# Front norms before the front's transposes, gt2's columns in the up loop, and the first merge products in the memory steps

## The reference

```
mod = silu(c) @ w_ada + b_ada                 -> shift, scale, gate (gt1, gt2) for two sub-layers
h   = rmsnorm(x) * (1 + sc1) + sh1
proj = h @ w_in + b_in                        -> xin, bg, cg, q, k, v, o, ig, fg, gate_c, gate_m
conv branch:   y = bg * dwconv3(cg * xin);  p_conv = y @ w_proj_conv
memory branch: mLSTM over chunks of 128, 4 heads (key 128, value 256), head norm, sigmoid(o) * hm,
               p_mlstm = ... @ w_proj_mlstm
z = sigmoid(gate_c) * p_conv + sigmoid(gate_m) * p_mlstm;   x = x + gt1 * (z @ w_out)
h = rmsnorm(x) * (1 + sc2) + sh2
x = x + gt2 * ((silu(dwconv3(h @ w_up_a)) * (h @ w_up_g)) @ w_down)     (d_ff = 2816)
out = rmsnorm(x) * g_final
```

## Time and profile before

| | us |
|---|---|
| median of 3 runs | 1341.28 (1341.21 to 1413.05) |
| profiled execution | 1341.2 |
| its span, core 2, the slowest | 1339.8 |
| spans of the eight cores | 1330.5 to 1339.8 |
| TensorE busy on core 2 | 1258.8 (94%) |
| VectorE, ScalarE busy | 679.4 (51%), 533.3 (40%) |

### The profile page before, as it was taken

The page is one execution under the profiler, slowest core; times in us unless marked ns, Lnnn a source line. Parts: engine busy times, 40 slices in busy tenths (PEclk is TensorE's granted clock), DMA queues, the critical chain, the costliest instruction groups (busy, mean ns, idle before and its releaser), DMA issues.

```text
span 1339.8 us, 21446 instructions; the slowest of 8 cores (1330.5 to 1339.8 us)
## 1 busy us (share of the span) xinstructions
PE 1258.8 (94%) x7694; PEld 689.0 (51%) x7694; DVE 679.4 (51%) x1241; ACT 533.3 (40%) x1069; POOL 86.1 (6%) x165
## 2 busy tenths in 40 slices
PE   1878999999899999999999999899999999999997
PEld 1445455666556655666654444445544444444443
DVE  1463342577733356666655423478632465655534
ACT  2554113765422235444443331566421255544212
POOL 3100000000100000000000000000000000000000
PEclk9998999999989999999999999999999999999999
DMA  8987025378684375334274673323627274432502
GB/s 140 163 206 122 0 40 94 54 114 135 104 188 64 63 146 107 64 63 80 40 182 75 159 145 63 64 32 64 134 56 126 44 139 77 88 64 41 101 16 110
DMA packets 35287, 126.19 MB, mean 94 GB/s; under 512 B 2796, under 2 KB 3052, under 8 KB 35184
## 3 DMA queue, kind: packets, MB, share of 16 engines
q0 software_dynamic: 27248, 97.93, 43.4%
q1 hardware_dynamic: 7936, 26.90, 5.8%
HBM read 214.34 MB, written 8.39 MB: 166 GB/s over the span
## 4 chain that ended last, share of the span: by engine, by line
PE 84%; DMA 6%; DVE 4%; issue 3%; ACT 2%; POOL 0%; DVEq 0%; ACTq 0%; SPq 0%; POOLq 0%
PE psum L548 56%; PE psum L1384 11%; PE psum L1231 4%; PE psum L890 4%; DMA arena<-xin 4%; PE psum L1500 2%; DVE arena L1079 1%; PE psum L507 1%; DMA xt<-xin 1%; DMA arena<-bada_row 1%; PE psum L753 1%; PE psum L952 1%; ACT sqj L458 1%; PE psum L954 0%; PE psum L963 0%
## 5 line engine op out<-in xcount | busy, mean ns | idle before, releaser
L548 PE MATMUL psum<-arena,wslot 128*128 128x512 bf16 (+1 forms) x4640 | 830.1, 338 | 7.7 <-DVE arena L1016 5.0
L548 PEld LDWEIGHTS psum<-arena,wslot 128*128 128x128 bf16 x4640 | 451.2, 98 | 356.8 <-issue 19.5
L1305 DVE SCALAR_TENSOR_TENSOR arena<-arena,pcol_t 128x1028 f32<-128x1028 f32 (+1 forms) x88 | 113.2, 1287 | 93.0 <-ACT arena L1302 88.5
L1384 PE MATMUL psum<-wslot,arena 128*128 128x512 bf16 x704 | 152.8, 379 | 1.7 <-ACT arena L528 1.7
L1167 ACT ACTIVATE arena<-psum,pcol_t 128x512 bf16<-128x512 f32 (+1 forms) x80 | 47.8, 603 | 162.6 <-PE psum L548 161.5
L1384 PEld LDWEIGHTS psum<-wslot,arena 128*128 128x128 bf16 x704 | 68.8, 98 | 84.0 <-issue 1.9
L1307 ACT ACTIVATE arena<-arena 128x1028 f32<-128x1028 f32 (+1 forms) x44 | 46.6, 1059 | 121.0 <-DVE arena L1305 121.0
L458 ACT ACTIVATE sqj<-arena 128x1024 bf16<-128x1024 f32 x40 | 42.2, 1055 | 93.2 <-DVE arena L1387 53.1
L1179 DVE TENSOR_TENSOR arena<-psum,arena 128x512 f32<-128x512 f32 (+1 forms) x40 | 23.4, 585 | 83.0 <-PE psum L548 82.1
L1231 PE MATMUL psum<-wslot,arena 128*128 128x512 bf16 (+1 forms) x272 | 60.3, 379 | 0.2 <-DVE arena L532 0.2
L890 PE MATMUL psum<-wslot,arena 128*128 128x512 bf16 (+1 forms) x272 | 59.3, 379 | 0.0
(11 more groups left out here) (201 smaller groups left out, 1095.9 us busy)
## 6 DMA issues: line engine op xcount, KB each, us to landing
wslot<-w_in POOLq DMA_DIRECT2D x32, 1024.0 KB, 11.9
arena<-xin SPq DMA_DIRECT2D x25, 512.0 KB, 16.4
wslot<-w_ada POOLq DMA_DIRECT2D x12, 1024.0 KB, 15.0
wslot<-w_up_a POOLq DMA_DIRECT2D x10, 1024.0 KB, 9.5
wslot<-w_up_g POOLq DMA_DIRECT2D x10, 1024.0 KB, 11.6
wslot<-w_down POOLq DMA_DIRECT2D x8, 1024.0 KB, 9.1
y<-arena SPq DMA_DIRECT2D x15, 512.0 KB, 2.7
wslot<-w_proj_conv POOLq DMA_DIRECT2D x4, 1024.0 KB, 13.9
```

The lines of the kernel that those rows point to most:

```text
L548: S.op("pe", lambda e: e.matmul(psum[:, b, 0:n], lhsT=wv[:, k, wcol0:wcol0 + 128], rhs=src[:, k, t0:t0 + n], start=(k == 0), stop=(k == 7) ...
L1305: S.op("dve", lambda e: e.scalar_tensor_tensor(out=t3[:, T0:NT], in0=a_s[:, s_ + T0:s_ + NT], scalar=pcol[:, cw + s_:cw + s_ + 1], in1=t3[ ...
L1384: S.op("pe", lambda e: e.matmul(psum[:, b, :], lhsT=act_t[jj][:, t0:t0 + 128], rhs=wv[:, jj % 8, :], start=(jj == 0), stop=(jj == NFF - 1) ...
```

## The change

Four moves; no product, evacuation or transfer of the computation is added or taken away.

1. Front: norms of the first stage's tiles are asked for later in the prefix loop (0 at c = 11 instead of 10, two each at c = 13 and 14), and inside an iteration behind `tgroup` rather than ahead of it. A fifth buffer `xfr` takes tile 8, so that all nine norms stand ahead of the three groups' transposes; `act_every` goes back to its default of 2 (four blocks of eight on each engine).
2. `sdb` is copied right after `stage_gates(0)` instead of after the prefix's gates.
3. gt2's two `ada_bcast` leave the units of the middle and run in the up loop after j = 6 and j = 10, with a bias buffer of their own. Row biases are loaded ahead: the first before the units (or at j = 1 of the up loop), the second right after the first is used.
4. `merge_conv(0)` and `merge_gate(0)` become units at the end of the chain, so the last chunk's D steps stand among them. `nblk` falls from 80 to 78 in the first stage, as the two `ada_bcast` left it, and stays 48 in the second.

```diff
-        def ada_bcast(n, dst, r_dst, half):
+        def load_bada(n, badabc, r_bada):
+            row0 = n % 2 * 512 + (0 if n < 6 else 1024)
+            S.dma("sp", badabc, badar_d[:, row0:row0 + 512].partition_broadcast(128), writes=[r_bada])
+
+        def ada_bcast(n, dst, r_dst, half, badabc=badabc, r_bada=r_bada):
             si = load_w("ada", n * T)
-            row0 = half * 512 + (0 if n < 6 else 1024)
-            S.dma("sp", badabc, badar_d[:, row0:row0 + 512].partition_broadcast(128), writes=[r_bada])
...
             free_w(si)
+            if half == 0:
+                load_bada(n + 1, badabc, r_bada)
...
-            t_, r_ = (xnb[f], r_xnb[f]) if f < 4 else (xfr[f - 4], r_xfr[f - 4]) if f < 8 else (xnb[0], r_xnb[0])
+            t_, r_ = (xnb[f], r_xnb[f]) if f < 4 else (xfr[f - 4], r_xfr[f - 4])
...
         for c in range(NPF):
-            norm_upto((0, 0, 0, 0, 0, 0, 0, 0, 0, 0, 1, 2, 3, 4, 5, 6)[c])
             sumsq(*squares.get(c, ()))
             if c in (3, 7, 11):
                 tgroup(c // 4 + 1)
+            norm_upto((0, 0, 0, 0, 0, 0, 0, 0, 0, 0, 0, 1, 2, 4, 6, 7)[c])
             b = kproj(c)
...
+            def merge_conv(j):
+                sg, zc, r_s, r_c = sg_t[j % 2], zc_t[j % 2], r_sg[j % 2], r_zc[j % 2]
+                if j == 0:
+                    S.reuse(r_sg + r_zc, [r_xs, r_u, r_t3] + r_sgf)
...
+                yield from proj_blocks(mt["gc"], (j % 4) * 128, hT, rd_h, tbs, merge_ev_g(j, 32))
+                yield from proj_blocks(mt["pc"], (j % 4) * 128, ycT, lambda k, t0, n: [r_yc[k]], tbs, ev_pc)
...
             S.reuse([r_bada], hooks["F"])
+            if first:
+                load_bada(4, badabc, r_bada)
             units = [unit_x(0), unit_c(0)]
             for j in range(1, 8):
-                units += [unit_x(j), unit_b(j - 1)] + ([unit_ada(j + 3)] if first else []) + [unit_c(j)]
-            units += ([unit_ada(11)] if first else []) + [unit_b(7)]
-            nblk = 24 * len(tbs) + (8 if first else 0)
+                units += [unit_x(j), unit_b(j - 1)] + ([unit_ada(j + 3)] if first and j < 7 else []) + [unit_c(j)]
+            units += [unit_b(7)]
+            units += [merge_conv(0), merge_gate(0)]
+            nblk = 24 * len(tbs) + (6 if first else 0)
...
-            for fn, j in [(merge_conv, 0), (merge_gate, 0), (merge_conv, 1), (merge_mem, 0), (merge_gate, 1), (merge_mem, 1)]:
-                fn(j)
+            drain(merge_conv(1))
+            merge_mem(0)
+            drain(merge_gate(1))
+            merge_mem(1)
...
                 if j == 1:
+                    if first:
+                        S.reuse([r_bada2], r_yc)
+                        load_bada(10, badabc2, r_bada2)
...
+                if first and j in (6, 10):
+                    i = (j - 6) // 4
+                    ada_bcast(10 + i, gt2bc, r_gt2, i, badabc2, r_bada2)
                 if j in (17, 19, 21):
                     dn_tile(0)
...
+        norm_upto(9)
         for g in range(3):
             tiles = front_tiles[g * 3:g * 3 + 3]
-            transp(tiles, hT, LAY[0][0][g * 3][0], r_h0[g], G1, r_G1, SH1, 3)
-            norm_upto(9)
+            transp(tiles, hT, LAY[0][0][g * 3][0], r_h0[g], G1, r_G1, SH1)
         allow_w(1 << 30, r_xt[xbuf[8]])
         stage_gates(0, r_h0)
+        r_sdb = Res("sdb")
+        S.reuse([r_sdb], [r_shbc])
+        S.op("dve", lambda e: e.tensor_copy(out=sdb, in_=...), reads=r_sdP, writes=[r_sdb])
```

More of the change, by code:

```diff
@@ L285, in _build @@
         shhl = sb("shhl", [128, 16], BF16)
-        xfr = [at("E", 8192 + i * 2048, [128, D], BF16) for i in range(4)]
+        xfr = [at("E", 8192 + i * 2048, [128, D], BF16) for i in range(4)] + [at("F", 20480, [128, D], BF16)]
         r_wslot = RL("wslot", NSLOT)
@@ L1108, in unit_ada, with drain, merge_ev_g, f @@
                 yield
+            def drain(*gens):
+                gens = list(gens)
+                while gens:
+                    for g_ in list(gens):
+                        try:
+                            next(g_)
+                        except StopIteration:
+                            gens.remove(g_)
+            r_sg, r_zc = RL("sg", 2), RL("zc", 2)
+            si_w = []
+            mt = {}
+            def merge_ev_g(j, col):
+                def f(b, t0, n):
+                    S.op("act", lambda e: e.activation(out=sg_t[j % 2][:, t0:t0 + n], in_=psum[:, b, 0:n], func=AF.Sigmoid,
+                                                       bias=pcol[:, PC_B + col + j:PC_B + col + j + 1]),
+                         reads=[r_bank[b], r_pc], writes=[r_sg[j % 2]])
+                return f
@@ new lines, in merge_gate @@
+            def merge_gate(j):
+                yield from proj_blocks(mt["gm"], (j % 4) * 128, hT, rd_h, tbs, merge_ev_g(j, 40))
+                if j in (6, 7):
+                    i = j - 6
+                    si_w.append(load_w("out", i * T))
+                    S.op("dve", lambda e: e.tensor_tensor(out=wslot[si_w[i]][:], in0=wslot[si_w[i]][:],
+                                                          in1=gt1bc[:, i * 512:(i + 1) * 512].rearrange("p (o n) -> p o n", o=1).to_broadcast([128, 8, 512]),
+                                                          op=ALU.mult), reads=[r_wslot[si_w[i]], r_gt1], writes=[r_wslot[si_w[i]]])
@@ new lines, in merge_mem, with ev_pm @@
+            def merge_mem(j):
+                sg, zc, r_s, r_c = sg_t[j % 2], zc_t[j % 2], r_sg[j % 2], r_zc[j % 2]
+                def ev_pm(b, t0, n):
+                    S.op("dve", lambda e: e.tensor_tensor(out=sg[:, t0:t0 + n], in0=psum[:, b, 0:n], in1=sg[:, t0:t0 + n], op=ALU.mult),
+                         reads=[r_bank[b], r_s], writes=[r_s])
+                    S.op("dve", lambda e: e.tensor_tensor(out=zT[:, j, t0:t0 + n], in0=sg[:, t0:t0 + n], in1=zc[:, t0:t0 + n], op=ALU.add),
+                         reads=[r_s, r_c], writes=[r_z[j][tbi(t0, n)[0]]])
+                proj(mt["pm"], (j % 4) * 128, sgoT, lambda k, t0, n: [r_hm[c] for c in hit(chunks, t0, n)], tbs, ev_pm)
+                if j % 4 == 3:
+                    free_w(mt["gm"], mt["pm"])
@@ L1162, in run_stage @@
             ask_res(0, 6)
[L1163 to L1183, removed]
-                    free_w(mt["gc"], mt["pc"])
-                if j == 7:
-                    ask_res(6, 8)
@@ L1252, in transp2 @@
                 yield from transp_blocks(tiles2[g], hT, chunks[groups[g][0]][0], r_h2[g], G2, r_G2, SH2)
-            def drain(*gens):
-                gens = list(gens)
-                while gens:
-                    for g_ in list(gens):
-                        try:
-                            next(g_)
-                        except StopIteration:
-                            gens.remove(g_)
             rest = list(groups[2])
@@ L1492, in _build @@
         r_MT, r_nsb, r_shn = RL("MT", 8), Res("nsb"), RL("shn", 2)
-        S.reuse(r_MT + [r_nsb] + r_shn, [r for i in range(2) for r in r_hTp[i]] + [r_shbc])
+        S.reuse(r_MT + [r_nsb] + r_shn, [r for i in range(2) for r in r_hTp[i]] + [r_shbc, r_xfr[4]])
         passes = [[(0, None), (1, 0), (2, 1), (3, 2), (4, 3)], [(5, 4), (6, 5), (7, 6), (0, 7)]]
```

48 lines of the change are left out of this document (17 added, 31 removed).

## The result

The changed kernel takes 1331.3 us (median of 4 runs, 1330.2 to 1332.9) against 1341.3 for the kernel before; the ratio is 0.9928, 95% interval 0.9916 to 0.9941, so 9.7 us less. The forecast was 14.9 us less, 1326.3. The measured time is inside the range given (1320 to 1335), and inside the 2% to which the chances referred; but the gain is two thirds of the sum: the terms of the front and of the memory steps were mis-sized, and `sdb` gave what was forecast only where TensorE's clock was low. Two of the four runs of the kernel before fell in the chip's slower state (1380.5 and 1413.1 us) and are left out of the ratio.

The account below looks back on a forecast made before the run. TensorE, nearly full behind the front, was taken as the bound, so only its idle time could be given back; VectorE ended the front. 5.5 + 0.6 + 6.7 + 2.1 = 14.9 us off 1341.2 gave 1326.3, range 1320 to 1335.

Parts of the forecast that it names:

- part 1: Front: later norms and three evacuations moved to ScalarE end it at 100.4 instead of 105.9 us, a gain of 5.5 us.
- the products for q start 0.4 us behind: End of the front: q's products follow VectorE's end by 0.4 us, as at 106.31 after 105.9 us before.
- part 4: First stage's middle: with `nblk` 78 for 80, TensorE's waits at memory steps fall from 8.0 to 6.0, gain 2.1 us.
- the wait at X of chunk 6: First stage's middle, a memory step: TensorE gets a wait of 0.8 us there in the new order.
- part 2: The `sdb` copy, moved ahead of the prefix gates, is covered by q's first products: 0.6 us gained, bounds 0 and 1.2.
- What bounds: Whole kernel: TensorE is nearly full behind the front, so only its idle time can be given back; VectorE ends the front.
- Part 3, the bias row: End of the middle: TensorE's 5.0 us wait goes, plus 1.7 for the clock, together 6.7 us.
- The bank count: End of the middle: banks come free in time for `unit_b(7)`, D steps and merge blocks, with 0.2 us to spare.
- The part 3 rival: End of the middle: VectorE still behind from the convolution, a 2 us wait and the clock's fall stay: 1329.9; chance 0.10.
- The front stays DMA-paced: Front: tiles 2 to 5 land no sooner, so it gives 0.9 instead of 5.5 us: 1330.9; chance 0.14.
- Four banks: Merge: each of 15 blocks waits 0.6 to 0.7 us for an evacuation, 10 us in all: 1336.3; chance 0.05.
- VectorE becomes the bound of the middle: Middle: every D waits 3.17 and every X 1.89 us, 40.5 where 8.0 were: 1360.9; chance 0.03.

Follow-up runs that it names:

- the weights held back: Changed kernel, but POOL asks for the next weights only after the front's last evacuation, not when the last x tile has landed: 0.9910 to the kernel before.
- the front alone: Kernel before with move 1 alone (norms later and behind the prefix's transposes, fifth buffer, evacuations shared 12 to 12): 0.9983.
- rows-ahead experiment: Kernel before with only the row biases loaded ahead and modulation unit 10 put ahead of 9: 0.9969.
- the last kernel: Changed kernel with late weights, norms behind `kevac`, and A, K and the root 0.04 of a chunk earlier in both stages: 0.9862 to the kernel before, 1323.5 us.
- the experiment with the old spacing: Changed kernel with the first stage's memory steps spread over 80 blocks instead of 78: 0.9931 to the kernel before.
- one tile for four: Changed kernel with one weight tile asked for when the last x tile has landed, the other three after the front's last evacuation: 0.9919 to the kernel before.

## Why the prediction was right and wrong, point by point

The steps that failed are these. In part 1 it is "the products for q start 0.4 us behind" VectorE: 5.5 us forecast, 3.5 measured on core 2, since TensorE stood there for its instructions. In part 4 it is the wait at X of chunk 6, where ScalarE's queue was not followed: 2.1 us forecast, a loss of 1.0 measured. In part 2 it is the cover of the copy, which is short by 0.9 us where TensorE runs at full clock.

**What bounds.** Right. TensorE's time behind the front passes on: out to down is the same but for the 3.46 us moved, and down to end within 0.8 us in the mean.

**Part 1, the front: 5.5 forecast, 3.5 on core 2, 2.5 in the mean.** VectorE's sum was right within 1 us: its work of 24.3 and its idle time of 3.0 gave an end at 100.4; to 99.8 it was busy 23.4 us and idle 3.3, and its last evacuation ended at 99.7. The failed step is "the products for q start 0.4 us behind it". Here 3.1 us lie between on core 2, and 2.7 to 3.9 on the seven cores with the pause, but 0.6 on core 4, which has none: TensorE's instruction block is late, and it was late in no row of before, where TensorE came to its place after it. With the weights held back q starts 0.8 us sooner in the mean, and on core 2 at 100.8, which is the forecast's 106.31 - 5.5; the ratio falls by 0.0018, 2.4 us, but that run's interval overlaps the changed kernel's. So of this term the pauses are shown and the microseconds only roughly. Means of q's start over several kernels with one front say the same: 105.5 for the old front (104.5, 105.5 and 106.5), 102.6 for the new one with the weights early (102.0, 102.8, 103.1 and 102.7), 101.4 with them held back (101.2 and 101.6). The Trainium skill (Runtime: NRT & Kernel Launch, Instruction fetch mechanics) says that instructions come in blocks of 16 KiB, fetched by DMA while the block before runs, and that the cost of crossing from one to the next is mostly hidden. The packets of 16 KB agree; that it stays hidden does not hold in this front, with 1.5 to 3.3 us between two products on seven of eight cores.

A second error is in taking core 2 for the chip. It had the latest q of all (106.31 against 102.85 to 105.42), so it had the most to gain, and the time is the slowest core's. After the change core 6 sets it, with 1329.6 for core 2's 1328.7.

**Part 2, sdb: 0.6.** Right for core 2, and not for the kernel as such: TensorE's wait before the state products is 2.06 us for 2.65, and no loss of cover shows there (the 0.9 for `gm_logf` in core 2's list is at 165.8 us, and stood there before). But it shows where q's products run at full clock (1.00 from q to state), which in the changed kernel is core 4 alone:

```profile
104.47 0.41 PE L583 MATMUL psum<-gm_logf,maskf 128*128 128x64 f32 x2 [0.89 <-DVE gm_logf L578]
```

This is VectorE's gate operation behind the copy. With the weights held back six cores wait so, 0.89 to 1.05 us. From q to state it is 25.88 us on core 4, where the front alone, with the copy in its old place, has 25.35 on four cores. So at full clock the move loses 0.5 us, outside the bounds of 0 and 1.2, and its 0.6 here is in part luck: q's products were slow because TensorE had just stood. No run puts the copy back in the kernels with the weights held back, where that should pay.

Not forecast either: core 2's first 24 q products took 6.35 us, over the 5.2 that the prediction named as a sign of being wrong, as more of them ran at the lower clock (granted clock 0.90 from q to state, 0.94 before; q to state 27.46 for 26.87), and its state to X lost the 1.7 us of a clock fall that it had had before (108.60 for 110.28). These two nearly cancel, and fall on other cores in other runs.

**Part 3, the bias row: 6.7.** Right in size on core 2: from the last D step to the first output product 119.1 us became 110.2 plus the one merge block of 1.73 that now precedes the last D, so 7.2. In the mean it is 5.6, as the other cores had waited 3.0 to 4.8 us and not 5.0. The bank count held, no merge block waited. The part 3 rival has its 2 us wait in the rows-ahead experiment, but the change took that too. The two products brought no gap of TensorE's in the up loop.

**Part 4, the steps: 2.1 forecast, minus 1.0 measured in waits.** TensorE's waits from 236 to 345 us went from 8.0 to 9.0. Step by step: D of chunk 3 2.77 (2.7 forecast), X of chunk 7 2.07 (1.9), X of chunk 2 and D of chunk 4 gone (as forecast), D of chunk 6 0.29 (0.3). What failed is X of chunk 6: 0.8 forecast, 1.10 + 1.50 measured. Smaller misses are two early steps of chunk 1, 0.44 and 0.58 where 0.3 was counted, and one more D step with 0.29. I had counted VectorE's queue and not ScalarE's. On core 2:

```profile
314.39 0.21 ACT L998 ACTIVATE sml<-sml 128x4 f32<-128x4 f32 x1 [6.90 <-DVE sml L996]
316.11 1.04 PE L553 MATMUL psum<-arena,wslot 128*128 128x258 bf16 x8 [1.10 <-ACT arena L1057]
319.09 0.27 PE L957 MATMUL psum<-arena 128*128 128x257 bf16 x1 [1.50 <-ACT arena L933]
```

The root of chunk 5 (L998) now stands behind a VectorE step that is behind the convolution; ScalarE waits 6.90 us for it, and behind it on ScalarE are the evacuation of `unit_x(5)`, for which TensorE waits 1.10, and K's, 1.50. Put ahead of the last `unit_c` block, as in the last kernel, both are gone.

The forecast also priced the steps by waits alone. Behind the 3.17 us of before the granted clock fell on four of the eight cores (0.87 in 312 to 325 us, 1.00 on the others), behind the 2.77 of the changed kernel it falls on all eight. At the 1.65 us that a fall costs in the experiment with the old spacing, I estimate this at another 0.8 us lost in the mean.

**Rivals.** "The front stays DMA-paced" was wrong: q came sooner. "Four banks", the rule of the Trainium skill on all eight PSUM banks (Perfetto Trace Analysis, Matmul Optimizations): no merge block on four banks waited, and with eight the kernel was not faster (0.9934 for 0.9928). "VectorE becomes the bound of the middle" did not come, 9.0 us against the 20.8 from which it decides.

**Sum, core 2.** Forecast 5.5 + 0.6 + 6.7 + 2.1 = 14.9. Measured 3.5 + 0.6 - 1.2 (q at the lower clock) + 1.7 (state) + 6.8 (middle and end together, 8.8 forecast) - 0.4 (down to end) = 11.0, span to span 11.1. From there to the 9.7 of the ratio it is other cores' turn to be slowest; the mean of the eight spans fell by 7.3 in the two profiled executions. That the total lies in the range says little for the terms: two came out smaller than forecast, and the bias row's full size is that of core 2, which had waited 5.0 us where the mean of the cores was 4.0.

## What to carry to other kernels

When the work of a step is moved in an order that every engine keeps, follow each engine's queue, also the third one's: the forecast was good to 0.2 us where I had followed VectorE, and off by 1.8 where ScalarE stood behind it. When work is moved under the cover of TensorE's products, work the cover out at both levels of its clock: here it held at the lower one and was 0.9 us short at the higher one. Price a wait together with the fall of the clock that can follow it. When a stretch is shortened, ask what arrives at a time of its own (here TensorE's instructions behind a burst of weights) and was hidden by the old length. And where the metric is the slowest of several cores, work out the term on a middle core as well; the slowest one's excess is not the change's to give.

## What was not expected of the hardware

TensorE's instruction blocks share the DMA engines with the kernel's own transfers: with 4 MB of weights in the queues one landed at 97.2 to 101.4 us and TensorE stood idle for it for up to 3.1 us; with the weights held back it landed at 93.4 to 98.9 us and TensorE had no gap over 0.46 us between the products. Its cause is shown by taking the weights away and by one tile for four, and by the landing times; what the block waits for within the engines isn't shown, and that the block is TensorE's is read from the times alone, since the queue's rows name no engine.
